# Sums of weight blocks for the second feed-forward matmul: added by transfers of GpSimd's queue in place of VectorE

## The reference

```python
h = modulate(rms_norm(x, g_pre_mlp), sh2, sc2)            # (512, 2048)
y = jnp.square(jax.nn.relu(h @ w_ff1)) @ w_ff2            # 2048 -> 8192 -> 2048
x = x + gt2 * rms_norm(y, g_post_mlp)
```

## Time and profile before

| | |
|---|---|
| runs | 2076.68, 2077.79 us (median 2077.23) |
| span of the profiled execution | 2076.6 us |
| TensorE busy | 2045.0 us (98%) |
| VectorE busy | 1599.3 us (77%) |
| ScalarE busy | 811.7 us (39%) |
| GpSimd busy | 87.7 us (4%) |
| feed-forward loop | about 798 to 2020 us of the span |

### The profile page before, as it was taken

One profiled execution on the slowest core, in us unless ns is written; L12 is line 12 of the kernel. 1 busy time (PEld: TensorE's weight loads), 2 busy tenths in 40 slices (PEclk: granted clock), 3 DMA queues, 4 the chain that ended last, 5 costly groups with the idle time before them and its releaser, 6 DMA issues.

```text
span 2076.6 us, 25311 instructions
## 1 busy us (share of the span) xinstructions
PE 2045.0 (98%) x9099; PEld 1670.2 (80%) x9099; DVE 1599.3 (77%) x1843; ACT 811.7 (39%) x1063; POOL 87.7 (4%) x97
## 2 busy tenths in 40 slices
PE   7999999999999999999999999999999999999998
PEld 5787788888778778888888888888888888888886
DVE  7999897776978787687686786776867867867767
ACT  6434622224543364334243343343342433433433
POOL 1001120000220001000000000000000000000000
PEclk9999999999999999999999999999999999999999
DMA  9986568856347843233332332332333323323335
GB/s 368 391 272 194 194 205 290 298 182 201 128 171 266 274 156 112 92 106 103 106 100 91 112 102 91 119 105 97 101 100 112 101 91 111 101 91 113 107 99 197
DMA packets 181600, 324.58 MB, mean 156 GB/s; under 512 B 12601, under 2 KB 49641, under 8 KB 179233
## 3 DMA queue, kind: packets, MB, share of 16 engines
q1 hardware_dynamic: 173600, 302.08, 44.0%
q0 software_dynamic: 3568, 16.95, 2.2%
q10 hardware_dynamic: 4368, 4.73, 0.7%
HBM read 313.20 MB, written 10.52 MB: 156 GB/s over the span
## 4 chain that ended last, share of the span: by engine, by line
PE 90%; DVE 7%; ACT 1%; issue 1%; DMA 0%; DVEq 0%; ACTq 0%
PE pair L939 11%; PE pair L940 11%; PE pair L941 11%; PE pair L964 9%; PE pair L965 9%; PE pair L966 9%; PE bank L568 5%; PE bank L570 5%; PE bank L569 5%; PE bank L580 3%; PE bank L582 3%; PE bank L581 3%; DVE acc L1581 1%; DVE w_lo L1549 1%; DVE stat L1766 1%
## 5 line engine op out<-in xcount | busy, mean ns | idle before, releaser
L2017 DVE TENSOR_TENSOR yg<-yg,pair 128x1024 f32<-128x1024 f32 x240 | 289.6, 1217 | 283.2 <-PE pair L966 283.2
L939 PE MATMUL pair<-h_hi,w_lo 128*128 128x512 f32 x1020 | 397.3, 390 | 0.0
L940 PE MATMUL pair<-h_lo,w_hi 128*128 128x512 f32 x1020 | 396.8, 389 | 0.0
L941 PE MATMUL pair<-h_hi,w_hi 128*128 128x512 f32 x1020 | 396.8, 389 | 0.0
L964 PE MATMUL pair<-w_hi,op_lo 128*128 128x512 f32 x840 | 328.3, 391 | 0.0
L965 PE MATMUL pair<-w_lo,op_hi 128*128 128x512 f32 x840 | 326.9, 389 | 0.0
L966 PE MATMUL pair<-w_hi,op_hi 128*128 128x512 f32 x840 | 326.9, 389 | 0.0
L1072 ACT ACTIVATE w_hi<-raw 128x1024 fp32r<-128x1024 f32 (+1 forms) x114 | 118.3, 1045 | 270.1 <-DMA raw<-in_w_in_dram 155.2
L939 PEld LDWEIGHTS pair<-h_hi,w_lo 128*128 128x128 f32 x1020 | 191.6, 188 | 39.9 <-issue 0.2
L941 PEld LDWEIGHTS pair<-h_hi,w_hi 128*128 128x128 f32 x1020 | 191.5, 188 | 39.9
L940 PEld LDWEIGHTS pair<-h_lo,w_hi 128*128 128x128 f32 x1020 | 191.5, 188 | 39.4
(11 more groups left out here) (295 smaller groups left out, 2803.0 us busy)
## 6 DMA issues: line engine op xcount, KB each, us to landing
raw<-in_w_ada_dram SPq DMA_DIRECT2D x128, 512.0 KB, 4.6
w_raw<-in_w_ff_dram SPq DMA_DIRECT2D x128, 512.0 KB, 3.8
raw<-in_w_ff_dram SPq DMA_DIRECT2D x128, 512.0 KB, 4.4
raw<-in_w_in_dram SPq DMA_DIRECT2D x74, 512.0 KB, 4.7
gst<-in_w_ada_dram SPq DMA_DIRECT2D x64, 512.0 KB, 7.8
raw<-in_w_out_dram SPq DMA_DIRECT2D x32, 512.0 KB, 4.8
x_tok<-in_x_dram SPq DMA_DIRECT2D x4, 1024.0 KB, 8.2
xr<-in_x_dram POOLq DMA_DIRECT2D x4, 1024.0 KB, 7.0
```

Source lines behind the costliest of these rows:

```text
L939: pe.matmul(b, lo[:, cols], h_hi[:, kt, :], start=(kt == 0), stop=False)
L940: pe.matmul(b, hi[:, cols], h_lo[:, kt, :], start=False, stop=False)
L941: last = pe.matmul(b, hi[:, cols], h_hi[:, kt, :], start=False, stop=(kt == KT - 1))
L2017: dve.tensor_tensor(y, y, pairs[2 + (i + r) % 2][:, :, :], ALU.subtract if i == 6 else ALU.add).then_inc(product_read, 1)
```

## The change

The four sums of a half are made by `dma_start(dst, src, accum_op=add)` on GpSimd's queue, from one SBUF buffer onto another. VectorE's `w2_total` is gone. As such a transfer can only add, the sums have other signs: chain = raw0 + raw1, chain + raw2, raw1 + raw2, chain + raw3. The signs of the left operands' sums S_1 and S_4 are turned with them, and product 2 is subtracted from its block and product 4 from one of its two blocks. `chain[0]` is `raw[:, 0]` itself, `chain[1]` is the buffer that was `w2_x`; block 0 of the second half is loaded into it. Each sum has a semaphore of its own, which ScalarE awaits. SP's waits on `w2_sum` become waits on `w2_lo` (`low_made`). Some semaphores outside this are merged (`norm_sum`, `norm_std`), one is dropped.

```diff
-        w2_x = acc[:, :, :].rearrange("p a b -> p (a b)")
+        chain = (raw[:, 0], acc[:, :, :].rearrange("p a b -> p (a b)"))
...
-                sp.dma_start(raw[:, which].rearrange("p (k n) -> p k n", k=2),
+                dst = raw[:, which] if which or last else chain[r]
+                sp.dma_start(dst.rearrange("p (k n) -> p k n", k=2),
...
-            sp.wait_ge(w2_sum, 1)
+            sp.wait_ge(acc_read, 24)
             load_w2((0, 0), 1, 0)
...
+                def low_made(n):
+                    sp.wait_ge(w2_lo, of((ck, 0), PRODUCTS, n + 1))
...
                 load_w1((ck, 1), 4)
-                sp.wait_ge(w2_sum, of((ck, 0), 8, 3))
+                low_made(4)
                 load_w2((ck, 0), 1, 2)
-                sp.wait_ge(w2_lo, of((ck, 0), PRODUCTS, 5))
                 load_w2((ck, 0), 1, 1)
                 w1_free(5)
                 load_w1((ck, 1), 5)
-                sp.wait_ge(w2_sum, of((ck, 0), 8, 4))
+                low_made(6)
                 load_w2((ck, 0), 1, 3)
                 w1_free(6)
                 load_w1((ck, 1), 6)
-                sp.wait_ge(w2_sum, of((ck, 0), 8, 5))
                 load_w2((ck, 1), 0, 0)
                 w1_free(7)
                 load_w1((ck, 1), 7)
-                sp.wait_ge(w2_sum, of((ck, 0), 8, 7))
+                low_made(11)
                 load_w2((ck, 1), 0, 2)
...
-                sp.wait_ge(w2_lo, of((ck, 0), PRODUCTS, 12))
                 load_w2((ck, 1), 0, 1)
...
-                sp.wait_ge(w2_sum, of((ck, 0), 8, 8))
+                low_made(13)
                 load_w2((ck, 1), 0, 3)
...
-                    sp.wait_ge(w2_sum, of((ck, 1), 8, 1))
                     load_w2((ck, 1), 1, 0)
...
             def w2_high(ck, n, first=False):
                 r, i = divmod(n, 7)
-                if i in SUM_OF:
-                    act.wait_ge(w2_sum, of(ck, 8, 4 * r + SUM_OF[i]))
-                    src = raw[:, 1] if i == 4 else w2_x
+                if i in w2_added:
+                    act.wait_ge(w2_added[i], of(ck, 32, 16 * (r + 1)))
+                    src = raw[:, 1] if i == 4 else chain[r]
...
-            def w2_total(ck, n, first=False):
...
                 if i == S_1:
-                    ins = dve.tensor_tensor(s, u_raw[:, 0:2, 256:512], u_block(A22), ALU.add)
+                    ins = dve.tensor_tensor(s, u_raw[:, 0:2, 256:512], u_block(A22), ALU.subtract)
...
                 elif i == S_4:
-                    ins = dve.tensor_tensor(s, u_block(A12), s, ALU.subtract)
+                    ins = dve.tensor_tensor(s, u_block(A12), s, ALU.add)
...
-            TARGETS = ([C11], [C22], [C12], [C12], [C21, C22], [C11], [C21])
+            TARGETS = ([(C11, ADD)], [(C22, ADD)], [(C12, SUB)], [(C12, ADD)], [(C21, ADD), (C22, SUB)], [(C11, ADD)], [(C21, ADD)])
...
-                    if n + 3 < PRODUCTS:
-                        if (n + 3) % 7 in SUM_OF:
-                            w2_total((ck, 0), n + 3)
-                    elif not last and n + 3 - PRODUCTS in SUM_OF:
-                        w2_total((ck, 1), n + 3 - PRODUCTS)
...
-            w2_total((0, 0), 1, first=True)
             w2_low((0, 0), 0)
             w1_low((0, 0), 8)
             w2_low((0, 0), 1)
-            w2_total((0, 0), 2)
...
             store_gate(7)
+            def add_block(ck, r, i):
+                n = 7 * r + i
+                pool.wait_ge(w2_lo, of(ck, PRODUCTS, {1: n, 2: n, 4: n - 2, 6: n - 3}[i]))
+                which = {1: 1, 2: 2, 4: 2, 6: 3}[i]
+                pool.wait_ge(w2_in[which], of(ck, 32, 16 * (r + 1)))
+                pool.dma_start(raw[:, 1] if i == 4 else chain[r], raw[:, which], accum_op=ALU.add).then_inc(w2_added[i], 16)
+            def sums(ck):
+                for r in range(2):
+                    for i in (1, 2, 4, 6):
+                        add_block(ck, r, i)
+            for ck in range(CHUNKS - 1):
+                sums((ck, 0))
             pool.wait_ge(gate_stored, 16 * 8)
```

More of the change, by code:

```diff
@@ L117, in hybrid_layer @@
     A11, S_1, S_2, S_4, S_3, A12, A22 = range(7)
-    SUM_OF = {1: 1, 2: 2, 4: 3, 6: 4}
     READS_BEFORE = [0, 1, 2, 3, 4, 6, 7]
@@ L321, in hybrid_layer @@
         first_half = sem("first_half")
-        w2_sum, w2_hi, w2_lo, product_done, product_read = (
-            sem(n) for n in ("w2_sum", "w2_hi", "w2_lo", "product_done", "product_read"))
+        w2_added = {i: sem(f"w2_added{i}") for i in (1, 2, 4, 6)}
+        w2_hi, w2_lo, product_done, product_read = (
+            sem(n) for n in ("w2_hi", "w2_lo", "product_done", "product_read"))
         relu_done, u_done, u_sum, op_hi_ready, op_lo_ready = (
@@ L328, in hybrid_layer @@
         x1r_in = sem("x1r_in")
-        f_ssq, y2_gated, fin_std, out_ready, stored = (sem(n) for n in ("f_ssq", "y2_gated", "fin_std", "out_ready", "stored"))
+        f_ssq, y2_gated, out_ready, stored = (sem(n) for n in ("f_ssq", "y2_gated", "out_ready", "stored"))
         XS, XR, RL, RA, YS, YR, X1S, X1R_, FS, FR, NM, ES, X1H, X1Q = 0, 4, 8, 12, 16, 32, 40, 44, 48, 64, 72, 80, 84, 92
@@ L419, in load_w1, with load_w2 @@
                              ).then_inc(w1_in[j % 2], 16)
-            def load_w2(ck, r, which):
+            def load_w2(ck, r, which, last=False):
                 half, side = ((0, 0), (0, 1), (1, 1), (1, 0))[which]
                 c0 = side * (D // 2) + r * COLS
-                sp.dma_start(raw[:, which].rearrange("p (k n) -> p k n", k=2),
+                dst = raw[:, which] if which or last else chain[r]
+                sp.dma_start(dst.rearrange("p (k n) -> p k n", k=2),
                              w_ff23[bass.ds(of(ck, 1, 0), 1), half * 2 * P:(half + 1) * 2 * P, c0:c0 + COLS].rearrange("c (k p) n -> p (c k) n", p=P)
@@ L542, in _ @@
                 sp.wait_ge(w2_lo, LAST * PRODUCTS + e + 1)
-                load_w2((LAST, 0), 1, which)
+                load_w2((LAST, 0), 1, which, last=True)
             for t in range(NT):
@@ L1388, in w2_high @@
                     act.wait_ge(w2_in[which], of(ck, 32, 16 * (r + 1)))
-                    src = raw[:, which]
+                    src = raw[:, which] if which else chain[r]
                 if first and n < 2:
@@ L1953, in w2_low @@
             def w2_low(ck, n):
-                i = n % 7
-                src = {0: raw[:, 0], 3: raw[:, 2], 4: raw[:, 1], 5: raw[:, 3]}.get(i, w2_x)
+                r, i = divmod(n, 7)
+                src = {3: raw[:, 2], 4: raw[:, 1], 5: raw[:, 3]}.get(i, chain[r])
                 dve.wait_ge(w2_hi, of(ck, PRODUCTS, n + 1))
@@ L1959, in w2_low @@
                 dve.tensor_tensor(w_lo[:, s], src, w_hi[:, s].bitcast(F32), ALU.subtract).then_inc(w2_lo, 1)
-            def w2_total(ck, n, first=False):
-                r, i = divmod(n, 7)
-                if not (first and n == 1):
-                    dve.wait_ge(w2_lo, of(ck, PRODUCTS, n - {1: 1, 2: 0, 4: 2, 6: 3}[i]))
-                if i == 1:
-                    for which in (0, 1):
-                        dve.wait_ge(w2_in[which], of(ck, 32, 16 * (r + 1)))
-                    ins = dve.tensor_tensor(w2_x, raw[:, 1], raw[:, 0], ALU.subtract)
-                elif i == 2:
-                    dve.wait_ge(w2_in[2], of(ck, 32, 16 * (r + 1)))
-                    ins = dve.tensor_tensor(w2_x, raw[:, 2], w2_x, ALU.subtract)
-                elif i == 4:
-                    ins = dve.tensor_tensor(raw[:, 1], raw[:, 2], raw[:, 1], ALU.subtract)
-                else:
-                    dve.wait_ge(w2_in[3], of(ck, 32, 16 * (r + 1)))
-                    ins = dve.tensor_tensor(w2_x, w2_x, raw[:, 3], ALU.subtract)
-                ins.then_inc(w2_sum, 1)
             def operand_low(ck, i):
@@ L2013, in read_product @@
                     dve.wait_ge(y2_zero, 1)
-                for th, side in TARGETS[i]:
+                for (th, side), sign in TARGETS[i]:
                     c0 = side * (D // 2) + r * COLS
                     y = y2[:, 2 * th:2 * th + 2, c0:c0 + COLS]
-                    dve.tensor_tensor(y, y, pairs[2 + (i + r) % 2][:, :, :],
-                                      ALU.subtract if i == 6 else ALU.add).then_inc(product_read, 1)
+                    dve.tensor_tensor(y, y, pairs[2 + (i + r) % 2][:, :, :], sign).then_inc(product_read, 1)
             def last_low(e):
```

23 lines of the change are left out of this document (12 added, 11 removed).

## The result

The changed kernel takes 2131.48 us (median of two runs, 2130.51 and 2132.45) against 2077.23 us: a ratio of 1.0263, 95% interval 1.0238 to 1.0288. It is slower by 54 us, where 32 were forecast; the time lies in the range given. The profiled execution has a span of 2130.7 us, 54.1 above the 2076.6 of before.

What follows compares the result with a forecast made beforehand. TensorE, 98% busy, was taken to bound the kernel. Turns 22 us plus start 9.5 us, together 32 us on the profiled 2076.6, gave 2108.6, with 0.6 for the runs' median 2109 us; range 2081 to 2195.

Steps and rivals of the forecast that it cites:

- What bounds the kernel: Feed-forward loop: TensorE is saturated, so VectorE's 146 us removed gain at most 3 us, from one weight-load wait.
- The chain and its budget: Turn between chunks: first wait may be 3.9 us, first two together 8.2; excess, less 0.2, stalls TensorE, 14 times.
- L: Time from a low part's end to ScalarE's start: landing plus 0.3 us wake; 4.7 first, 5.3 second in a turn.
- The price D1: First adding transfer of a turn: 4.4 us from issue to landing, taken from a 1,024 KB store.
- The price D2: Second adding transfer of a turn: 0.6 us more than the first's 4.4, for weight loads issued just behind it.
- The start: Start of the loop: TensorE stops for 5.1 us plus one landing of 4.4, 9.5 us.
- L + L: Blocks 8 and 9, second column half: two successive waits for sums, free up to 11.7 us, a loss 15 times above.
- Signs: Additions for subtractions of the same shape: cost nothing.
- SP's queue: Weight buffers released at the low part instead of the sum, over 15 us cover against 4.4 us landing: cost nothing.
- blocks 4 and 6: Their sums are wanted two products later than they can be added, 11 us and more of cover: free.
- The plain price: Rival: adding hidden in the write, landings 3.1 and 3.7 us, no stall at the turn, 2082 us; chance 0.18.
- The slower accumulate: Rival: adding transfer paid in three passes, landings 5.7 and 6.3 us, slower by over 2%, 2152 us; chance 0.28.

Runs made afterwards that it cites:

- plain-copy run: Changed kernel with each of GpSimd's 120 transfers a plain copy of the same 512 KB, nothing added: 2087.54 us, ratio 1.0055.
- moving the follower: Changed kernel with the sum of block 4 (and 11) issued only after block 2's (9's) low part: 2131.65 us, ratio 1.0264.
- the kernel with the start moved: Changed kernel, GpSimd's first sum ahead of clearing y, block 1's high and low parts behind the first left operands: 2114.03 us, ratio 1.0178.
- the spare buffer: Changed kernel with block 0 also loaded into a second buffer, onto which the next chunk's first sum is added early: 2091.84 us, ratio 1.0075.

## Why the prediction was right or wrong

**What bounds the kernel: right.** VectorE gave back 136.5 us and nothing came of it; in the plain-copy run it is as idle and the turn is TensorE's 81.60. The 146 us forecast added up the sums' own durations, 1.22; neighbours on VectorE start 1.14 us apart, and 120 x 1.14 is 137.

**The chain and its budget: right.** Slack of 8.2 and the 0.2 of before put a turn with the measured L at 4.82 + 5.93 - 8.4 = 2.35; 2.42 were measured. With the loads away it gives 4.82 + 4.85 - 8.4 = 1.27 against 83.10 - 81.77 = 1.33. With 256 KB, L1 + L2 is 3.62 + 4.07 = 7.7, below 8.2, and nothing stalls. Without the first landing nothing stalls either.

**The price D1: right.** 4.42 where I took 4.4. That it fits to 0.02 us is luck in part: I had it from a store to HBM of twice the bytes. The reason holds as far as the bytes go: they cost 2.4 us per 512 KB added, where the plain copy's 2.86 is 1.1 above the 1.8 of the smallest row. That is the rule of the Trainium skill (Collectives: The Full Stack, The bandwidth ceiling), about half the rate of a copy, and these runs agree with it. That the second input is what costs the bytes is argued, not shown. The estimate of 3.2 us by the Trainium skill (DMA: Bandwidth & Descriptors, Anatomy of one DMA) is near the plain 2.86 and 1.2 us short for the adding transfer.

**The price D2: the step that failed.** I wrote "For the second transfer of a turn I add 0.6". It was 1.1 us more: 5.54. I had read 0.6 off loads that go out in pairs; that row says nothing of what two loads do to an adding transfer. L2 was 5.93 in place of 5.3, which with L1's 0.1 makes a turn 2.4 in place of 1.6: 34 us in place of 22, 12 of the missing 22. The cause, the two loads beside it, was named rightly and is shown by moving them away (1.1 us a turn gained) and by moving the follower (nothing). The same loads cost the plain copy 0.05 us; it has landed 1.9 us after the first of them goes out, where the sum is under way for 4.5.

**The start: right, with one term left out.** 9.5 forecast, 9.53 measured from the clear on, and TensorE is 9.5 us late at the third block of its first piece, as the argument has it. Behind that its matmuls still start 0.43 us apart until 807.5, at the lower level of the clock, and lose 0.8 more. In the total 2.9 of it do not show, since the part before the loop ran that much earlier in this execution.

**What the sum left out: disturbed turns, 12.6 us.** The prediction let 14 equal turns stand. The largest is the last, 6 us, from a late GpSimd issue that lets SP's loads go first, and from the clock behind the stop. The same lateness at the 61st sum is block 8's, which I had costed at nothing: L + L was to be up to 11.7, and with the wake at 1.04 and a landing of 7.5 us it costs 2.3 us, once in 15. In the 14 other chunks products 8 and 9 wait for nothing, as forecast. The first turn has a landing of 6.2 us. One turn lost 2.1 us, 0.5 through a landing of 5.9 and 1.6 through the clock (below). The risk "a granted clock that falls when TensorE stops" was listed without a price; it came to 4.5 us, a fifth of the 22 that the sum lacked.

**Signs, SP's queue, blocks 4 and 6: right.** Turns of 81.60 with all of it in place.

**Rivals.** The plain price is excluded by the landing of 4.42 against 2.86. The slower accumulate decided from L1 + L2 = 10.6 and 2118 us on: L1 + L2 is 10.75, so by its own mark that case came, at its low end and mostly by contention, not by three passes. With those 10.75 its formula gives 14 x 2.35 + 9.7 = 43 us; the rest to 54 are the disturbed turns. The single time most favoured, 2109, and the case "within 2%" (0.57) did not come; "slower by over 2%" had 0.41. The time lies in the stated range because the range took in that rival.

## What to carry to other kernels

Before work is moved from an engine with slack to a transfer, ask who reads the result next: off the chain six of eight sums were free, in it two cost 2.4 us a chunk. Price a transfer in a chain together with what other queues issue right behind it, and ask what happens if its own issue comes a microsecond late, behind them. A stall of a few tenths on an operand is better looked for in the order of the engine that makes it: two lines moved gained what 120 transfers did not.

## What the runs showed of the hardware

- An adding SBUF to SBUF transfer of 512 KB lands in 4.42 us alone, 256 KB in 3.22, a plain copy of 512 KB in 2.86. GpSimd spends 0.86 us on its issue, 0.53 on a plain one.
- Two 512 KB loads issued 1.0 and 1.6 us behind it make it 1.1 us longer (5.54), the sum of 256 KB 0.45, the plain copy 0.05. Issued 1.7 and 1.2 us ahead of a plain copy, they made it 1.6 us longer (4.54). A second adding transfer on its own queue, 0.53 us behind, does nothing to it, and lands itself 9.8 us after its issue, 4.8 after the first.
- GpSimd is sometimes late by 0.7 to 1.4 us with an adding issue for which all is there. It was so at the 61st, 114th and 118th sum in the changed kernel, and one sum later in the kernels that had something else between its first and second sum. Four memsets ahead of all did not move it. With plain copies the 61st and the 118th were on time, and the 114th was late by 2.7 us.
- TensorE's clock after stops. The matmuls behind one of the turns' stops:

```profile
1326.29 0.74 PE L964 MATMUL pair<-w_hi,op_lo 128*128 128x512 f32 x1 [1.98 <-DVE op_lo L1965]
1326.82 0.63 PE L965 MATMUL pair<-w_lo,op_hi 128*128 128x512 f32 x1
```

and three stretches of the changed kernel: behind the stop at the start, that one, and behind the long stop of the last turn (columns as in the earlier trace rows):

```profile
802.95:807.55 4.60, 4.57 (x11) 3.45 (x12) 1.62 (x3) 3.78 (x5) 1.76 (x2) 0.50 0.62 119
1326.20:1330.20 4.00, 3.91 (x10) 3.11 (x11) 3.06 (x4) 2.52 (x3) 0.51 (x1) 0.57 0.96 236
2008.00:2012.40 4.40, 4.40 (x10) 3.44 (x11) 3.54 (x5) 2.52 (x3) 0.45 (x1) 0.50 0.60 119
```

The matmuls start 0.43 us apart for 3.5 to 4.5 us, where 0.2267 is usual: the lower of the clock's two levels, 1.2 GHz, after which it is back at 2.4. It was so behind every stop of 4.3 to 8.3 us in the loops of all these kernels, twelve of them. Behind shorter ones it differs: one of 2.14 us (the one above) and one of 2.06 (the kernel with the start moved, at 888.96) have it, one of 2.31 (897.34 here) and one of 3.55 (the spare buffer, at 1968.02) have not, nor has any stop of a turn under 2 us. The other kernels with such turns had a distance of 84.4 where this one has 86.31. What makes one short stop differ from the next stays open.
